# Split weights stored woven in pairs of k-tiles, and strip matmuls run from the last column to the first

## The chip, the core and the metric

The kernel runs on one core of one Trainium2 chip. The metric is the device time of one launch in microseconds. The core has a matmul engine (TensorE, PE in the rows; its weight loads are listed apart as PEld), VectorE (DVE), ScalarE (ACT), GpSimd (POOL) and SyncE (SP), which issues most of the transfers. All share the on-chip memory SBUF; matmuls write to PSUM.

## The reference, cut to what matters

The kernel computes one step of a hybrid decoder layer for 272 prompt rows (256 and 16 meta rows in front) and 8 sample rows, in float32:

```
h = rmsnorm(x, norm1_g);  z = h @ w_in                      # 2048 x 16400 weights
a_out = bg * causal_dwconv(cg * u);  b_out = sigmoid(o) * mlstm(q, k, v, gates)
x = x + (sigmoid(g_a) * a_out + sigmoid(g_b) * b_out) @ w_out
h2 = rmsnorm(x, norm2_g)
up = causal_dwconv(h2 @ w_up)                               # 2048 x 11264 weights
x = x + (silu(up[..., D_FF:]) * up[..., :D_FF]) @ w_down    # 5632 x 2048 weights
y = rmsnorm(x, norm_f_g)
```

Nearly all work is in the four weight products. Each weight element is used for 264 to 280 columns (tokens).

## The kernel before, in words

Every product is cut into **strips**: 128 output features for all tokens, accumulated in one PSUM bank (`bank[0]` to `bank[3]`). A strip's weights come in **units** of up to 8 k-tiles of 128x128 (`KU` = 8; in the down product a strip is 8, 8 and 6 k-tiles). Four units are in flight: `w_raw`, `w_hi` and `w_lo` have four slots of 8·128 columns each (`RING` = 4).

A unit goes through three steps. SP loads it into its slot of `w_raw` (`load`, waits until the unit that was four before has its `w_lo`). ScalarE rounds it to the matmul's reduced format, fp32r, into `w_hi` (`split_hi`, waits for the load and for `unit_used`, that is, until TensorE has finished the unit four before). VectorE subtracts and writes the rest to `w_lo` (`split_lo`). The tokens are split in the same way into `xh`/`xl`, `mh`/`ml` or `hh`/`hl`. TensorE then does, for each k-tile of the unit, hi weights with hi tokens (L1520), then for each hi weights with lo tokens (L1524), then lo weights with hi tokens (L1528): 24 matmuls for a unit of 8 (`unit`). Each matmul has a weight load of 128 columns of its own.

In `w_hi` and `w_lo` a k-tile is 128 adjacent columns, as in `w_raw`; the token tiles are read from column `c0` up, and the bank is written from column 0 up.

The stages in order: a prologue of about 34 us with the first units, which other engines than usual split (`first_hi`, `first_lo_part` on TensorE, L1028 and L1035 on VectorE, L489 and L493 on GpSimd, L730 and L731 on ScalarE); 8 heads of 16 strips of `w_in`, each with a `front` (280 columns for three strips) and a `back` (268 columns); 16 strips of `w_out` (266); then twice 44 strips of `w_up` (268) and 16 strips of `w_down` (264). VectorE also empties the banks (`take`, L987) and does the convolutions; its instructions run in the order in which they are written, with `step` calls for the weights put between the others. Nothing is scheduled by a planner: the order on every engine is written out by hand.

Of the kernel before, what the change touches and what calls it, by code (L numbers as in the profile page):

```python
# [6 lines left out]
def hybrid_decoder_step(nc, ins, outs, scratch_rows, scratch_v, scratch_q):  # L7
# [10 lines left out]
    f32, f32r = mybir.dt.float32, mybir.dt.float32r  # L18
    ALU, ACT = mybir.AluOpType, mybir.ActivationFunctionType
# [7 lines left out]
    P = 128  # L27
# [9 lines left out]
    KT = D // P  # L37
    FT = DFF // P
    TP = NMETA + SEQ
    NT = TP + NS  # L40
# [25 lines left out]
    KU = 8  # L66
# [37 lines left out]
    with ctx:  # L104
        def sb(name, shape, dt=f32):
            return ctx.enter_context(nc.sbuf_tensor(name, shape, dt))

        def sem(name):
            return ctx.enter_context(nc.semaphore(name))
# [3 lines left out]
        xh = sb("xh", [P, KT, NT], f32r)  # L113
        xl = sb("xl", [P, KT, NT], f32r)
        w_raw = sb("w_raw", [P, RING, KU * P])
        w_hi = sb("w_hi", [P, RING, KU * P], f32r)
        w_lo = sb("w_lo", [P, RING, KU * P], f32r)
# [173 lines left out]
        bank = [ctx.enter_context(nc.psum_tensor(f"strip{i}", [P, 512], f32)) for i in range(RING)]  # L291
# [4 lines left out]
        hi_done = sem("hi_done")  # L296
# [6 lines left out]
        half_hi, first_lo, mp_done, bias_done = sem("half_hi"), sem("first_lo"), sem("mp_done"), sem("bias_done")  # L303
# [61 lines left out]
        def col(c, j):  # L365
            return vecs[:, bass.ds(c * KT + j, 1)]


        @block.sync
        def _(sp):  # L370
# [100 lines left out]
        def _(g):  # L471
# [14 lines left out]
            g.memset(gws[:, :, :].bitcast(f32), 0.0).then_inc(gw_split, 1)  # L486
            g.wait_ge(hi_done, 2)
            g.wait_ge(first_lo, 1)
            g.tensor_tensor(w_lo[:, 2, :], w_raw[:, 2, :], w_hi[:, 2, :].bitcast(f32), ALU.subtract)\  # L489
             .then_inc(first_lo, 1)  # L490
            for i, u in enumerate((1, 3)):
                g.wait_ge(hi_done, i + 3)
                g.tensor_tensor(w_lo[:, u, :], w_raw[:, u, :], w_hi[:, u, :].bitcast(f32), ALU.subtract)\  # L493
                 .then_inc(lo_done, 2)

            g.wait_ge(gates_in, 16)
# [152 lines left out]
            for m in range(KT):  # L649
# [5 lines left out]
                if m < NQ:  # L655
                    p = slice(m * Q, (m + 1) * Q)
# [48 lines left out]
        def _(act):  # L705
            def split_hi(u, slot, n16):
                act.wait_ge(unit_landed[slot], n16)
                act.wait_ge(unit_used, u + 1)
                act.activation(w_hi[:, slot, :], w_raw[:, slot, :], ACT.Copy).then_inc(hi_done, 1)  # L709

            def step(n, per, base_u, i):

                u4 = n * per + (base_u + i + RING)
                split_hi(u4, i % RING, n * (16 * per // RING) + 16 * ((base_u + i) // RING + 2))
# [9 lines left out]
            for k in range(KT):  # L724
                act.wait_ge(x_turned, k + 1)
                act.activation(xh[:, k, :], x_bank[k % 6][:, 0:NT], ACT.Copy, scale=vecs[:, k:k + 1])\
                 .then_inc(xh_done, 1)
                if k == 3:
                    act.wait_ge(unit_landed[0], 16)
                    act.activation(w_hi[:, 0, 0:KU * P // 2], w_raw[:, 0, 0:KU * P // 2], ACT.Copy).then_inc(half_hi, 1)  # L730
                    act.activation(w_hi[:, 0, KU * P // 2:], w_raw[:, 0, KU * P // 2:], ACT.Copy).then_inc(hi_done, 1)  # L731
                for kept in (k - 2, k) if k % 4 == 3 else ():
                    act.wait_ge(xl_done, kept + 1)
                    act.activation(xres[:, kept, :], x_bank[kept % 6][:, 0:NT], ACT.Copy).then_inc(x_copied, 1)
                if k == 7:
                    act.wait_ge(hi_done, 2)
                    split_hi(1, 1, 16)
# [237 lines left out]
        def _(v):  # L975
            def split_lo(u, slot):
                v.wait_ge(hi_done, u + 1)
                v.tensor_tensor(w_lo[:, slot, :], w_raw[:, slot, :], w_hi[:, slot, :].bitcast(f32),  # L978
                                ALU.subtract).then_inc(lo_done, 1)

            def step(n, per, base_u, i):
                split_lo(n * per + (base_u + i + RING), i % RING)
# [35 lines left out]
            for k in range(KT):  # L1018
                v.wait_ge(xh_done, k + 1)
                v.scalar_tensor_tensor(out=xl[:, k, :], in0=x_bank[k % 6][:, 0:NT], scalar=vecs[:, k:k + 1],  # L1020
                                       in1=xh[:, k, :].bitcast(f32), op0=ALU.mult, op1=ALU.subtract)\
                                        .then_inc(xl_done, 1)
                if k % 2 == 1:
                    v.tensor_copy(xres[:, k - 1, :], x_bank[(k - 1) % 6][:, 0:NT]).then_inc(x_kept, 1)
                if k == 3:
                    v.wait_ge(half_hi, 1)
                    v.wait_ge(hi_done, 1)
                    v.tensor_tensor(w_lo[:, 0, :], w_raw[:, 0, :], w_hi[:, 0, :].bitcast(f32), ALU.subtract)\  # L1028
                     .then_inc(first_lo, 1)
                if k in (3, 11):  # L1030
                    u = 2 if k == 3 else 3
                    v.wait_ge(unit_landed[u], 16)
                    if k == 11:
                        v.wait_ge(hi_done, 3)
                    v.tensor_scalar(w_hi[:, u, :], w_raw[:, u, :], 1.0, None, ALU.mult).then_inc(hi_done, 1)  # L1035
            v.wait_ge(lo_done, RING + 4)
            v.wait_ge(ssq_done, 3)
            v.wait_ge(msq_clear, 1)
# [358 lines left out]
        def _(pe):  # L1397
# [43 lines left out]
            def first_hi(s, lo, hi):  # L1441
                c0 = C0 if s == 0 else 0
                for k in range(lo, hi):
                    if s == 0 and k == 0:
                        pe.wait_ge(half_hi, 1)
                    elif k % KU == 0 or (s == 0 and k == 4):
                        pe.wait_ge(hi_done, 1 + s + 2 * (k // KU))
                    pe.wait_ge(xl_done, k + 1)
                    w = slice(k % KU * P, (k % KU + 1) * P)
                    for t, xt in enumerate((xh, xl)):  # L1450
                        mm = pe.matmul(bank[s][:, 0:NT - c0], w_hi[:, 2 * s + k // KU, w], xt[:, k, c0:NT],  # L1451
                                       start=(k == 0 and t == 0), stop=False)
                return mm

            def first_lo_part(s, lo, hi, last=False):
                c0 = C0 if s == 0 else 0
                h = lo // KU
                if h == 0:
                    pe.wait_ge(first_lo, s + 1)
                else:  # L1460
                    pe.wait_ge(lo_done, RING + 2 * (s + 1))
                for k in range(lo, hi):
                    pe.wait_ge(xh_done, k + 1)
                    mm = pe.matmul(bank[s][:, 0:NT - c0], w_lo[:, 2 * s + h, (k - h * KU) * P:(k - h * KU + 1) * P],  # L1464
                                   xh[:, k, c0:NT], start=False, stop=(last and k == KT - 1))
                return mm

            def gates(lo, hi):
# [6 lines left out]
            turn_x(0, 4)  # L1475
            warm(6)
            first_hi(0, 0, 4)
            turn_x(4, 8)
            first_lo_part(0, 0, 4)
            first_hi(1, 0, 4)  # L1480
            first_hi(0, 4, 6)
            first_lo_part(0, 4, 8)
            first_hi(0, 6, 8).then_inc(unit_used, 1)
            first_lo_part(1, 0, 4)
            turn_x(8, 12)
            first_hi(1, 4, 8)
# [24 lines left out]
            def unit(u, slot, b, k0, kk, rh, rl, c0, c1, first, last, waits=(), frees=1):  # L1511


                pe.wait_ge(hi_done, u + 1)
                for k in range(kk):
                    for at_k, sm, value in waits:
                        if at_k == k:
                            pe.wait_ge(sm, value)
                    w = slice(k * P, (k + 1) * P)
                    pe.matmul(bank[b][:, 0:c1 - c0], w_hi[:, slot, w], rh[:, k0 + k, c0:c1],  # L1520
                              start=(first and k == 0), stop=False)
                for k in range(kk):
                    w = slice(k * P, (k + 1) * P)
                    pe.matmul(bank[b][:, 0:c1 - c0], w_hi[:, slot, w], rl[:, k0 + k, c0:c1], start=False, stop=False)  # L1524
                pe.wait_ge(lo_done, u + 1 + RING)
                for k in range(kk):
                    w = slice(k * P, (k + 1) * P)
                    mm = pe.matmul(bank[b][:, 0:c1 - c0], w_lo[:, slot, w], rh[:, k0 + k, c0:c1],  # L1528
                                   start=False, stop=(last and k == kk - 1))
                if frees:  # L1530
                    mm.then_inc(unit_used, frees)
# [226 lines left out]
```

## Time and profile before

| | us |
|---|---|
| median of 3 runs | 1708.52 |
| lowest, highest | 1707.7, 1710.4 |
| span of the profiled execution (first to last instruction) | 1706.3 |
| TensorE busy in it | 1695.1 |
| VectorE busy in it | 1200.1 |
| ScalarE busy in it | 766.5 |
| GpSimd busy in it | 479.6 |

The profiled execution has no time of its own beside its span; the median of the runs is 2.2 us above that span. A matmul's row spans its whole way through the engine, so rows of neighbours overlap; the distance from start to start tells what one costs in a stream.

### The profile page before, as it was taken

The page shows a single profiled execution, that of the slowest core. Times are in us where ns is not written, and L with a number is a line of the kernel's source. Part 1 is how long each engine was busy: PE and PEld are TensorE (multiplying, and loading weights), DVE is VectorE, ACT ScalarE, POOL GpSimd, SP SyncE. Part 2 cuts the span into 40 slices and gives each one's busy share as a digit, 9 for nine tenths or more (in the row PEclk, how much of TensorE's full clock was granted, in tenths as well). Part 3 has the DMA queues.
Part 4 walks back from the last instruction along what each step waited for, and adds up shares of the span by engine and source line. Part 5 has one row for each costly group of instructions (what it writes and reads, how often), then busy time and mean ns, then how long its engine had stood idle before and what let it go on. Part 6 is the DMA issues. An engine that isn't in the chain of part 4 may idle for free.

```text
span 1706.3 us, 37177 instructions
## 1 busy us (share of the span) xinstructions
PE 1695.1 (99%) x13726; PEld 1688.7 (99%) x13726; DVE 1200.1 (70%) x1901; ACT 766.5 (45%) x916; POOL 479.6 (28%) x501
## 2 busy tenths in 40 slices
PE   9999999999999999999999999999999999999997
PEld 8999999999999999999999999999999999999997
DVE  5875957667595766759688877777555777777554
ACT  6545435354443535444444554544333334334443
POOL 4422414242141424215343222222000222222220
PEclk9999999999999999999999999999999999999999
DMA  8787786868778586877866666656666666666663
GB/s 204 183 230 197 201 212 155 225 162 231 188 198 212 156 226 163 230 189 199 196 178 182 185 175 175 180 173 173 183 181 181 181 178 179 176 180 177 183 176 119
DMA packets 591165, 318.80 MB, mean 187 GB/s; under 512 B 17684, under 2 KB 585988, under 8 KB 588988
## 3 DMA queue, kind: packets, MB, share of 16 engines
q1 hardware_dynamic: 578564, 292.99, 63.2%
q10 hardware_dynamic: 10448, 21.57, 4.7%
q0 software_dynamic: 2064, 2.92, 0.8%
q8 instruction: 72, 1.18, 0.3%
q14 instruction: 17, 0.14, 0.0%
HBM read 305.09 MB, written 12.78 MB: 186 GB/s over the span
## 4 chain that ended last, share of the span: by engine, by line
PE 99%; ACT 0%; POOL 0%; DVE 0%; issue 0%; ACTq 0%; POOLq 0%; DVEq 0%
PE strip L1528 32%; PE strip L1520 32%; PE strip L1524 32%; PE aux L1399 1%; PE aux L1407 1%; PE strip L1451 0%; PE aux L1581 0%; PE aux L1471 0%; PE strip L1464 0%; PE aux L1611 0%; PE aux L1610 0%; PE aux L1624 0%; PE strip L1399 0%; PE aux L1615 0%; PE aux L1608 0%; PE aux L1616 0%
## 5 line engine op out<-in xcount | busy, mean ns | idle before, releaser
L978 DVE TENSOR_TENSOR w_lo<-w_raw,w_hi 128x1024 fp32r<-128x1024 f32 x556 | 723.1, 1303 | 315.3 <-ACT w_hi L709 314.8
L709 ACT ACTIVATE w_hi<-w_raw 128x1024 fp32r<-128x1024 f32 x557 | 586.1, 1059 | 756.7 <-PE strip L1528 724.7
L1520 PE MATMUL strip<-xh,w_hi 128*128 128x268 f32 (+1 forms) x3424 | 493.1, 286 | 0.0
L1528 PE MATMUL strip<-xh,w_lo 128*128 128x268 f32 (+1 forms) x3424 | 492.4, 286 | 0.0
L1524 PE MATMUL strip<-xl,w_hi 128*128 128x268 f32 (+1 forms) x3424 | 492.0, 286 | 0.0
L1528 PEld LDWEIGHTS strip<-xh,w_lo 128*128 128x128 f32 x3424 | 449.4, 188 | 0.3
L1520 PEld LDWEIGHTS strip<-xh,w_hi 128*128 128x128 f32 x3424 | 449.4, 188 | 0.2
L1524 PEld LDWEIGHTS strip<-xl,w_hi 128*128 128x128 f32 x3424 | 449.4, 188 | 0.0
L680 POOL TENSOR_TENSOR gg<-sg,cz 128x264 f32<-128x264 f32 x44 | 57.1, 1297 | 415.8 <-ACT sg L923 415.8
L1520 PE MATMUL strip<-hh,w_hi 128*128 128x264 f32 x704 | 102.2, 286 | 0.0
L683 POOL TENSOR_TENSOR hid<-gg,cz 128x264 f32<-128x264 f32 x44 | 73.5, 1670 | 102.2 <-DVE cz L1327 102.2
L1528 PE MATMUL strip<-hh,w_lo 128*128 128x264 f32 x704 | 101.3, 285 | 0.0
L1524 PE MATMUL strip<-hl,w_hi 128*128 128x264 f32 x704 | 101.2, 284 | 0.0
L1528 PEld LDWEIGHTS strip<-hh,w_lo 128*128 128x128 f32 x704 | 92.2, 189 | 0.0
L1524 PEld LDWEIGHTS strip<-hl,w_hi 128*128 128x128 f32 x704 | 91.9, 188 | 0.0
L1520 PEld LDWEIGHTS strip<-hh,w_hi 128*128 128x128 f32 x704 | 91.7, 188 | 0.0
L620 POOL TENSOR_TENSOR so<-so,sbm 128x266 f32<-128x266 f32 x16 | 20.6, 1287 | 137.1 <-ACT sbm L881 137.1
L987 DVE TENSOR_TENSOR zs<-strip,rbc 128x266 f32<-128x266 f32 x88 | 38.0, 431 | 26.6 <-PE strip L1528 26.6
L1319 DVE SCALAR_TENSOR_TENSOR cz<-zs,vecs,cz 128x256 f32<-128x256 f32 x88 | 42.7, 485 | 12.9 <-DVE cz L1316 1.8
L611 POOL TENSOR_TENSOR c_st<-c_st,kv 128x512 f32<-128x512 f32 x32 | 49.5, 1545 | 6.5 <-ACT c_st L864 4.5
L606 POOL TENSOR_TENSOR kv<-vg,qkd_g 128x512 f32<-128x512 f32 x32 | 49.2, 1538 | 2.6 <-DMA vg<-scratch_v 0.6
L1327 DVE SCALAR_TENSOR_TENSOR cz<-zs,vecs,cz 128x256 f32<-128x256 f32 x88 | 42.7, 485 | 6.0
(324 smaller groups left out, 1285.3 us busy)
## 6 DMA issues: line engine op xcount, KB each, us to landing
w_raw<-in_w_in SPq DMA_DIRECT2D x256, 512.0 KB, 4.4
w_raw<-in_w_up SPq DMA_DIRECT2D x176, 512.0 KB, 3.9
w_raw<-in_w_down SPq DMA_DIRECT2D x64, 512.0 KB, 3.9
w_raw<-in_w_out SPq DMA_DIRECT2D x32, 512.0 KB, 4.4
w_raw<-in_w_down SPq DMA_DIRECT2D x32, 384.0 KB, 3.3
out<-c_st ACTq DMA_DIRECT2D x8, 1024.0 KB, 7.2
c_st<-in_state_mlstm_C ACTq DMA_DIRECT2D x7, 1024.0 KB, 10.5
rb<-scratch_rows ACTq DMA_DIRECT2D x8, 270.0 KB, 5.0
```

Source lines behind the costliest of these rows:

```text
L606: g.tensor_tensor(kv[:, :, :], vg[:, :].unsqueeze(1).broadcast_to([P, 2, DV]), kw_p.unsqueeze(2).broadcast_to([P, 2, DV]), ALU.mult).then_ ...
L611: g.tensor_tensor(c_p, c_p, kv[:, :, :], ALU.add).then_inc(c_updated, 1)
L680: g.tensor_tensor(gg[:, :], sg[:, :], cz[:, 0, :], ALU.mult).then_inc(gg_done, 1)
L683: g.tensor_tensor(hid[:, :], gg[:, :], cz[:, 1, :], ALU.mult).then_inc(hid_done, 1)
L709: act.activation(w_hi[:, slot, :], w_raw[:, slot, :], ACT.Copy).then_inc(hi_done, 1)
L978: v.tensor_tensor(w_lo[:, slot, :], w_raw[:, slot, :], w_hi[:, slot, :].bitcast(f32), ALU.subtract).then_inc(lo_done, 1)
L987: v.tensor_tensor(out, bank[b][:, c0 - from_c:c0 - from_c + width], rbc[:, c0:c0 + width], ALU.mult).then_inc(evacuated, 1)
L1319: v.scalar_tensor_tensor(out=cz[:, z, 0:SEQ], in0=zs[:, z, 1:1 + SEQ], scalar=wcol[1], in1=cz[:, z, 0:SEQ], op0=ALU.mult, op1=ALU.add)\
L1327: v.scalar_tensor_tensor(out=cz[:, z, 0:SEQ], in0=zs[:, z, 0:SEQ], scalar=wcol[0], in1=cz[:, z, 0:SEQ], op0=ALU.mult, op1=ALU.add)\
L1520: pe.matmul(bank[b][:, 0:c1 - c0], w_hi[:, slot, w], rh[:, k0 + k, c0:c1], start=(first and k == 0), stop=False)
L1524: pe.matmul(bank[b][:, 0:c1 - c0], w_hi[:, slot, w], rl[:, k0 + k, c0:c1], start=False, stop=False)
L1528: mm = pe.matmul(bank[b][:, 0:c1 - c0], w_lo[:, slot, w], rh[:, k0 + k, c0:c1], start=False, stop=(last and k == kk - 1))
```

## The change

Two edits of layout and of order inside instructions, neither of which adds, removes or moves an instruction: each engine's list has the same length and order as before (1568 instructions as written for TensorE, 724 for VectorE, 407 for ScalarE, 230 for GpSimd, 291 for SyncE, loops counted once).

1. **Woven weights.** In `w_hi` and `w_lo` two neighbouring k-tiles share 256 columns: the even k-tile has the even columns, the odd one the odd columns. Whoever writes them (ScalarE, VectorE, at the start GpSimd) writes each k-tile with a step of 2 elements, which is 8 bytes, and reads `w_raw` in sequence as before. VectorE and GpSimd also read `w_hi` with step 2. TensorE loads each weight tile with step 2.
2. **Descending strips.** In every strip matmul the moving rows (the tokens) are read from the last column to the first, and the output is written from the last column to the first, both with a step of -1.

Transfers, `w_raw`, all other matmuls and all waits stay. The diff, cut where lines repeat the pattern:

```diff
+        def plain(t, slot, k0=0, k1=KU):
+            return t[:, slot, k0 * P:k1 * P].rearrange("p (j e n) -> p j e n", e=2, n=P)
+
+        def woven(t, slot, k0=0, k1=KU):
+            return t[:, slot, k0 * P:k1 * P].rearrange("p (j n e) -> p j e n", e=2, n=P)
+
+        def weights(t, slot, k):
+            return t[:, slot, k // 2 * 2 * P:(k // 2 + 1) * 2 * P].rearrange("p (n e) -> p e n", e=2)[:, k % 2, :]
...
@@ split_hi, on ScalarE
-                act.activation(w_hi[:, slot, :], w_raw[:, slot, :], ACT.Copy).then_inc(hi_done, 1)
+                act.activation(woven(w_hi, slot), plain(w_raw, slot), ACT.Copy).then_inc(hi_done, 1)
...
@@ split_lo, on VectorE
-                v.tensor_tensor(w_lo[:, slot, :], w_raw[:, slot, :], w_hi[:, slot, :].bitcast(f32),
+                v.tensor_tensor(woven(w_lo, slot), plain(w_raw, slot), woven(w_hi, slot).bitcast(f32),
                                 ALU.subtract).then_inc(lo_done, 1)
...
@@ the prologue, on VectorE (the splits on GpSimd and ScalarE there alike)
-                    v.tensor_scalar(w_hi[:, u, :], w_raw[:, u, :], 1.0, None, ALU.mult).then_inc(hi_done, 1)
+                    v.tensor_scalar(woven(w_hi, u), plain(w_raw, u), 1.0, None, ALU.mult).then_inc(hi_done, 1)
...
@@ unit, on TensorE (first_hi and first_lo_part alike)
-                    w = slice(k * P, (k + 1) * P)
-                    pe.matmul(bank[b][:, 0:c1 - c0], w_hi[:, slot, w], rh[:, k0 + k, c0:c1],
+                    pe.matmul(bank[b][:, 0:c1 - c0][:, ::-1], weights(w_hi, slot, k), rh[:, k0 + k, c0:c1][:, ::-1],
                               start=(first and k == 0), stop=False)
...
-                    mm = pe.matmul(bank[b][:, 0:c1 - c0], w_lo[:, slot, w], rh[:, k0 + k, c0:c1],
+                    mm = pe.matmul(bank[b][:, 0:c1 - c0][:, ::-1], weights(w_lo, slot, k), rh[:, k0 + k, c0:c1][:, ::-1],
                                    start=False, stop=(last and k == kk - 1))
```

## Rows read from the trace of the kernel before

**Rows 1.** The page, part 1: busy time, share of the span, instructions.

```profile
PE 1695.1 (99%) x13726; PEld 1688.7 (99%) x13726; DVE 1200.1 (70%) x1901; ACT 766.5 (45%) x916; POOL 479.6 (28%) x501
```

**Rows 2.** The page, part 4: the chain that ended last, by engine.

```profile
PE 99%; ACT 0%; POOL 0%; DVE 0%; issue 0%; ACTq 0%; POOLq 0%; DVEq 0%
```

**Rows 3.** Timeline of PE, second w_up stage: start, length, what, count.

```profile
1500.63 1.14 PE L1528 MATMUL strip<-xh,w_lo 128*128 128x268 f32 x8
...
1503.56 1.14 PE L1528 MATMUL strip<-xh,w_lo 128*128 128x268 f32 x8
```

**Rows 4.** Timeline of PE, first w_up stage, the same work.

```profile
1000.29 1.16 PE L1528 MATMUL strip<-xh,w_lo 128*128 128x268 f32 x8
...
1003.27 1.16 PE L1528 MATMUL strip<-xh,w_lo 128*128 128x268 f32 x8
```

**Rows 5.** Groups by line and shape, PEld: count, busy us, mean ns of one.

```profile
L1524 PEld LDWEIGHTS strip<-xl,w_hi 128*128 128x128 f32 x3424 | 449.4, 188 | 0.0
...
L1528 PEld LDWEIGHTS strip<-hh,w_lo 128*128 128x128 f32 x704 | 92.2, 189 | 0.0
...
L1528 PEld LDWEIGHTS strip<-mh,w_lo 128*128 128x128 f32 x256 | 33.2, 188 | 0.0
...
L1399 PEld LDWEIGHTS aux<-ident,xg 128*128 128x128 f32 x32 | 4.1, 142 | 0.0
...
L1581 PEld LDWEIGHTS aux<-q_t,tails 128*16 128x16 f32 x16 | 0.9, 94 | 1.2
```

**Rows 6.** Timeline, end of the run: weight loads for matmuls of one column.

```profile
1694.75 0.75 PEld L1708 LDWEIGHTS aux<-ones,acc 128*128 128x128 f32 x6
```

**Rows 7.** The page, part 5: the two splits, busy us, mean ns.

```profile
L978 DVE TENSOR_TENSOR w_lo<-w_raw,w_hi 128x1024 fp32r<-128x1024 f32 x556 | 723.1, 1303 | 315.3 <-ACT w_hi L709 314.8
L709 ACT ACTIVATE w_hi<-w_raw 128x1024 fp32r<-128x1024 f32 x557 | 586.1, 1059 | 756.7 <-PE strip L1528 724.7
```

**Rows 8.** Groups by line and shape, ACT: a split of half the size.

```profile
L731 ACT ACTIVATE w_hi<-w_raw 128x512 fp32r<-128x512 f32 x1 | 0.6, 642 | 0.0
```

**Rows 9.** Line L978 alone: duration ns, minimum, median, maximum.

```profile
L978 DVE TENSOR_TENSOR w_lo<-w_raw,w_hi x556: 1183/1225/2873, 32.5 to 1685.6; 128x1024 fp32r<-128x1024 f32 x186
```

**Rows 10.** Groups by line and shape, DVE: stepped and unstepped small ones.

```profile
L1313 DVE TENSOR_SCALAR up_last<-zs 128x10 f32 x88 | 15.7, 178 | 13.1 <-DVE zs L987 3.7
...
L1323 DVE TENSOR_TENSOR cz<-cz,pre_f 128x8 f32<-128x8 f32 x88 | 14.1, 160 | 0.0
...
L1015 DVE TENSOR_REDUCE sel<-ident 128x8 f32<-128x128 f32 x1 | 0.4, 383 | 2.8 <-POOL tails L484 2.8
...
L1363 DVE TENSOR_TENSOR x<-strip,xres 128x128 f32<-128x128 f32 x1 | 0.3, 292 | 7.2 <-PE strip L1528 7.2
```

**Rows 11.** Windows, all engines: heads, w_out, second w_up; busy us of each engine.

```profile
330.00:846.00 516.00, 516.00 (x4180) 514.69 (x4179) 362.36 (x508) 232.19 (x295) 169.89 (x185) 1.00 0.76 195
850.00:900.00 50.00, 50.00 (x413) 50.00 (x412) 41.35 (x56) 21.10 (x26) 20.53 (x21) 1.00 0.70 186
...
1310.00:1560.00 250.00, 250.00 (x2050) 250.00 (x2050) 197.27 (x385) 96.79 (x106) 66.20 (x42) 1.00 0.61 178
```

**Rows 12.** The same windows, busy time of L978 alone.

```profile
330.00:846.00 516.00, 225.91 (x166) 1.00 0.76 195
850.00:900.00 50.00, 24.04 (x17) 1.00 0.70 186
...
1310.00:1560.00 250.00, 103.34 (x85) 1.00 0.61 178
```

**Rows 13.** The page, part 6: the weights' transfers, KB each, us from issue to landing.

```profile
w_raw<-in_w_in SPq DMA_DIRECT2D x256, 512.0 KB, 4.4
```

**Rows 14.** Line L1035, the split on DVE in the prologue.

```profile
L1035 DVE TENSOR_SCALAR w_hi<-w_raw x2: 685/688/690, 13.8 to 22.3; 128x1024 fp32r<-128x1024 f32 x2
```

**Rows 15.** Timeline of POOL in the prologue: the split after it.

```profile
14.61 2.39 POOL L489 TENSOR_TENSOR w_lo<-w_raw,w_hi 128x1024 fp32r<-128x1024 f32 x1 [10.39 <-DVE w_hi L1035]
```

**Rows 16.** The chain, prologue: the matmuls that take that split.

```profile
18.12 0.52 PE strip L1464 x4
```

More of the change, by code:

```diff
@@ L488, in _ @@
             g.wait_ge(first_lo, 1)
-            g.tensor_tensor(w_lo[:, 2, :], w_raw[:, 2, :], w_hi[:, 2, :].bitcast(f32), ALU.subtract)\
+            g.tensor_tensor(woven(w_lo, 2), plain(w_raw, 2), woven(w_hi, 2).bitcast(f32), ALU.subtract)\
              .then_inc(first_lo, 1)
@@ L492, in _ @@
                 g.wait_ge(hi_done, i + 3)
-                g.tensor_tensor(w_lo[:, u, :], w_raw[:, u, :], w_hi[:, u, :].bitcast(f32), ALU.subtract)\
+                g.tensor_tensor(woven(w_lo, u), plain(w_raw, u), woven(w_hi, u).bitcast(f32), ALU.subtract)\
                  .then_inc(lo_done, 2)
@@ L729, in _ @@
                     act.wait_ge(unit_landed[0], 16)
-                    act.activation(w_hi[:, 0, 0:KU * P // 2], w_raw[:, 0, 0:KU * P // 2], ACT.Copy).then_inc(half_hi, 1)
-                    act.activation(w_hi[:, 0, KU * P // 2:], w_raw[:, 0, KU * P // 2:], ACT.Copy).then_inc(hi_done, 1)
+                    act.activation(woven(w_hi, 0, 0, KU // 2), plain(w_raw, 0, 0, KU // 2), ACT.Copy).then_inc(half_hi, 1)
+                    act.activation(woven(w_hi, 0, KU // 2), plain(w_raw, 0, KU // 2), ACT.Copy).then_inc(hi_done, 1)
                 for kept in (k - 2, k) if k % 4 == 3 else ():
@@ L1027, in _ @@
                     v.wait_ge(hi_done, 1)
-                    v.tensor_tensor(w_lo[:, 0, :], w_raw[:, 0, :], w_hi[:, 0, :].bitcast(f32), ALU.subtract)\
+                    v.tensor_tensor(woven(w_lo, 0), plain(w_raw, 0), woven(w_hi, 0).bitcast(f32), ALU.subtract)\
                      .then_inc(first_lo, 1)
@@ L1448, in first_hi @@
                     pe.wait_ge(xl_done, k + 1)
-                    w = slice(k % KU * P, (k % KU + 1) * P)
                     for t, xt in enumerate((xh, xl)):
-                        mm = pe.matmul(bank[s][:, 0:NT - c0], w_hi[:, 2 * s + k // KU, w], xt[:, k, c0:NT],
+                        mm = pe.matmul(bank[s][:, 0:NT - c0][:, ::-1], weights(w_hi, 2 * s + k // KU, k % KU), xt[:, k, c0:NT][:, ::-1],
                                        start=(k == 0 and t == 0), stop=False)
@@ L1463, in first_lo_part @@
                     pe.wait_ge(xh_done, k + 1)
-                    mm = pe.matmul(bank[s][:, 0:NT - c0], w_lo[:, 2 * s + h, (k - h * KU) * P:(k - h * KU + 1) * P],
-                                   xh[:, k, c0:NT], start=False, stop=(last and k == KT - 1))
+                    mm = pe.matmul(bank[s][:, 0:NT - c0][:, ::-1], weights(w_lo, 2 * s + h, k - h * KU),
+                                   xh[:, k, c0:NT][:, ::-1], start=False, stop=(last and k == KT - 1))
                 return mm
@@ L1518, in unit @@
                             pe.wait_ge(sm, value)
-                    w = slice(k * P, (k + 1) * P)
-                    pe.matmul(bank[b][:, 0:c1 - c0], w_hi[:, slot, w], rh[:, k0 + k, c0:c1],
+                    pe.matmul(bank[b][:, 0:c1 - c0][:, ::-1], weights(w_hi, slot, k), rh[:, k0 + k, c0:c1][:, ::-1],
                               start=(first and k == 0), stop=False)
                 for k in range(kk):
-                    w = slice(k * P, (k + 1) * P)
-                    pe.matmul(bank[b][:, 0:c1 - c0], w_hi[:, slot, w], rl[:, k0 + k, c0:c1], start=False, stop=False)
+                    pe.matmul(bank[b][:, 0:c1 - c0][:, ::-1], weights(w_hi, slot, k), rl[:, k0 + k, c0:c1][:, ::-1], start=False, stop=False)
                 pe.wait_ge(lo_done, u + 1 + RING)
                 for k in range(kk):
-                    w = slice(k * P, (k + 1) * P)
-                    mm = pe.matmul(bank[b][:, 0:c1 - c0], w_lo[:, slot, w], rh[:, k0 + k, c0:c1],
+                    mm = pe.matmul(bank[b][:, 0:c1 - c0][:, ::-1], weights(w_lo, slot, k), rh[:, k0 + k, c0:c1][:, ::-1],
                                    start=False, stop=(last and k == kk - 1))
```

## The prediction

> **What bounds the kernel now.** I read the shares of busy time first [rows 1]: TensorE is at 99%, VectorE at 70%, ScalarE at 45%. The chain that ended last says the same from the other side, 99% of it is TensorE [rows 2]. So every nanosecond of a strip matmul counts at once, and what the other engines do counts only if it makes TensorE wait.
>
> How long is one strip matmul in the stream? In the second w_up stage 24 of them, one unit, take 1503.56 - 1500.63 = 2.93 us, which is 122.1 ns each, for 268 columns [rows 3]. In the first w_up stage the same work takes 2.98 us or 124.2 ns [rows 4]. There are 3 x (3424 + 704 + 256) = 13,152 strip matmuls outside the prologue, one weight load each [rows 5]; at 122 to 124 ns they fill 1,606 to 1,633 us of the span of 1706.3. One nanosecond on each is 13.2 us, 0.8% of the time. The granted clock is 1.00 throughout, the 2.4 GHz level [rows 11]. At that level 268 columns at one per cycle are 111.7 ns, so 10.4 ns of the 122.1 are something else.
>
> **The edits on TensorE.** Three streams of its change: the weight load (step 2), the moving read (step -1) and the bank write (step -1). No row of before shows any of them with such a step, so each is bounded.
>
> Weight load. It takes 188 ns for 128 columns and 94 ns for 16 [rows 5]: (188 - 94)/112 = 0.84 ns a column, 107 ns for a tile. It isn't limited by what the memory gives: in the transposes the same 128 columns of 4 bytes take 142 ns, (142 - 94)/112 = 0.43 ns a column [rows 5]. In the strips the load thus takes words at half the rate at which that port can deliver adjacent ones. With a step of 2 half of what is fetched goes unused, and the half that is left is just the rate needed. Lower bound 0. Upper bound: a column costs twice as much, 107 ns more. Loads in a row without long matmuls stand (750 - 189)/5 = 112 ns apart [rows 6], 10 ns under the 122.1 of a strip matmul; so the first 10 ns of any growth are hidden and the rest is not: 112 + 107 - 122 = 97 ns each, 13,152 times, +1,276 us. I take 0, because of the reserve of a factor of two, and keep the other as a rival.
>
> Moving read and bank write. Here no reserve shows: they run at 268 columns in 122.1 ns. Adjacent words stay adjacent, all spans have even lengths (264, 266, 268, 280) and start at even columns, so that any aligned pair of words that was fetched or written together is still a pair, met in the other order. Lower bound 0. Upper bound: pairs are no longer joined and a column costs two cycles, 111.7 ns more, 13,152 times, +1,469 us. I take 0, as the set of words touched in each pair of columns is the same; between the ends there is no row to lean on, so this is the largest single risk.
>
> The Trainium skill speaks against this edit: "PSUM — Partial Sum Buffer", Specifications, has cachelines of 8 bytes in PSUM and says that any non-contiguous access pattern slows matmuls significantly. If a step of -1 counts as non-contiguous there, the time is that of the upper bound. No row of this trace shows a bank written with a step.
>
> **The edits on ScalarE and VectorE.** Per unit ScalarE writes 1024 woven elements: 1059 ns, and 642 for 512 [rows 7, 8], (1059 - 642)/512 = 0.81 ns an element. If a stepped write doubles that, a split takes 1.89 us; 557 of them add 463 us and ScalarE stands at 1,230 of 1,706 us, still not the bound. It waits 725 us for TensorE to free slots [rows 7], and a slot turns round in 4 x 2.93 = 11.7 us, against 1.06 + 1.23 + 4.4 us for hi, lo and the next transfer [rows 7, 9, 13]. Even with 1.89 + 1.95 + 4.4 = 8.2 us there are 3.5 us to spare. So: nothing on the path, whichever bound holds. What hides it is the four slots.
>
> VectorE reads one woven stream and writes another: 1,225 ns at the median [rows 9]. Lower bound of the change 0. Two rows of before have steps. The reduction L1015 reads 128 elements at a step of 32 bytes in 383 ns, where 128 adjacent ones take 292 ns in L1363: 0.71 ns an element more [rows 10], which makes a split 1.95 us. L1313 writes 10 elements at a step of 384 bytes in 178 ns, where 8 adjacent ones take 160 in L1323: (178 - 160 - 2)/10 = 1.6 ns more, 2.86 us a split [rows 10]. How much can VectorE bear? In the second w_up stage it is busy 197.3 of 250 us, 103.3 of that in 85 splits [rows 11, 12]; the rest, 94 us, leaves (250 - 94)/85 = 1.83 us for a split. In the w_out stage (50 - 17.3)/17 = 1.92 us, in the heads (516 - 136.5)/166 = 2.29 us. So up to 1.83 us nothing happens, and that is the point from which this decides.
>
> I take 0 here too. A step of 8 bytes touches every 16 bytes twice, the stepped rows above touch each piece of 32 bytes or more once; only in the latter does each word cost an access of its own for certain. The Trainium skill has both sides. "SBUF — State Buffer", section "Door 1: The DMA port swizzle", gives cachelines of 16 bytes and full bandwidth with at least two hits in each: by it a step of two floats is free for all engines. "Vector Engine (DVE) Microarchitecture Reference", section 5.2, measured that runs must be two adjacent words on an 8-byte boundary, 1.71 to 1.98 ns per column otherwise; an estimate from it is 1.98 x 1.024 + 0.16 = 2.2 us a split, over every budget above except the heads'. The trace has no row with a step of 8 bytes that would settle it.
>
> **The prologue.** L1035 splits 1024 elements in 688 ns [rows 14], faster per element than L978, a rate that a stepped write may lose; then it takes about 1.23 us, 0.54 more, twice. GpSimd's split behind the first one starts at 14.61 and takes 2.39 us [rows 15]: 0.54 later it ends at 17.5, and TensorE takes its result at 18.12 [rows 16]. Nothing. If GpSimd's three splits also double, TensorE waits about 2 us for each, 5 us at most. I take 0.
>
> **Sum.** 0 + 0 + 0 + 0 against the span of 1706.3 and the 2.2 us that lie around it up to the median of the runs: 1708.5 us. Its own range: the one variation of the stream that the trace shows without any change of shape is the 2.1 ns between [rows 3] and [rows 4]. Should the first w_up stage (44 strips of 48 matmuls) lose it, that is -4.4 us; should all others gain it, 11,040 x 2.1 ns = +23 us. So 1,704 to 1,732.
>
> **The rivals.**
>
> *Descending streams aren't joined in pairs* (slower). Place: every strip matmul, stage by stage alike. Price 111.7 ns each, 1708.5 + 1,469 = 3,178 us; it decides from the first nanosecond, as nothing hides it. For it: no reserve in the stream, and the page on PSUM. Against it: the words of a pair stay the same. 0.14.
>
> *Woven weights halve the load* (slower): 1708.5 + 1,276 = 2,985 us. For it: the load is only 10 ns from being the limit. Against it: the transposes' rate. 0.03.
>
> *VectorE becomes the bound* (slower). Place: the w_up stages first, then w_out. With 1.95 us a split, (1.95 - 1.83) x 4 splits x 44 pairs of strips = 21 us, and its in-order waits there, which would come on top, are at most about as much again; w_out 1 us: 1,730 to 1,755, say 1,745. With 2.2 us: 65 + 9 us and the waits, up to 1,810. The far end, 2.86 us, would be 181 us in w_up, 146 in the heads and some 50 elsewhere, 2,090. For it: two streams with a step on the engine that has the least room. Against it: two words of every 16 bytes are used. 0.13.
>
> *The 10.4 ns above the column rate come from streams that disturb each other, and the new orders part them* (faster). If half go, 5.2 x 13,152 = -68 us, 1,640 us. For it: they are there, and they differ by stage. Against it: nothing says that order matters. 0.03.
>
> **How the numbers follow.** My forecast, no stream that counts is slower, has 0.67. A difference of 0.2%, 3.4 us, is about what a measurement can tell from none; it is 0.26 ns on a matmul. Within the forecast I give 0.50 to less than that, 0.11 to slower and 0.06 to faster. With the rivals: same 0.50, slower 0.11 + 0.14 + 0.03 + 0.13 = 0.41, faster 0.06 + 0.03 = 0.09. The predicted time is 1708.5. The range holds the forecast and the rival on VectorE up to its 2.2 us, and leaves out the two large losses and the gain, 0.20: 1,697 to 1,812.
>
> **What would show it.** Right: units of 24 matmuls still 2.93 us in the second w_up stage, weight loads still 188 ns, L978 near 1.23 and L709 near 1.06 us, chain 99% TensorE. Weight loads at about 295 ns show the second rival. Units of about 5.6 us with loads still at 188 ns show the first. L978 above 1.83 us, TensorE idle behind it in w_up and the granted clock perhaps falling there show the third. L978 between 1.3 and 1.8 us with unchanged time would mean that the step costs and room hid it. What would make the prediction wrong is above all a cost per column in the descending streams, for which the trace before offers no row at all.

## The result: 5 us slower, all of it in the stream of strip matmuls

| | before | after |
|---|---|---|
| median, us (8 runs each) | 1709.29 | 1714.09 |
| lowest to highest | 1707.7 to 1710.4 | 1713.04 to 1714.43 |
| span of the profiled execution | 1706.3 | 1712.3 |
| ratio of the runs | | 1.0029, 95% interval 1.0019 to 1.0039 |

The forecast was no change, 1708.5. The loss is small, but clear of it: the interval doesn't reach 1. Executions of the kernel before have spans from 1705.6 to 1709.1 us, so the span of one profiled execution can be up to 3 us off from the next; the profiled one here, 1706.3, is a low one, and the runs put the loss at 4.8 us. The page of the changed kernel, busy time and chain, answers to [rows 1, 2]:

```profile
PE 1701.1 (99%) x13726; PEld 1694.7 (99%) x13726; DVE 1199.0 (70%) x1901; ACT 838.9 (49%) x916; POOL 481.3 (28%) x501
...
PE 99%; ACT 0%; POOL 0%; DVE 0%; issue 0%; ACTq 0%; POOLq 0%; DVEq 0%
```

TensorE gained 6.0 us of busy time and the span 6.0 us; it still waits for nobody to speak of. So the question is what a matmul costs in the stream. The timelines of TensorE in the second and the first w_up stage, which answer to [rows 3, 4] (start, length, line, shape, count):

```profile
1500.68 1.15 PE L1533 MATMUL strip<-xh,w_lo 128*128 128x268 f32 x8
...
1503.63 1.03 PE L1533 MATMUL strip<-xh,w_lo 128*128 128x268 f32 x7
```

```profile
1000.98 1.15 PE L1533 MATMUL strip<-xh,w_lo 128*128 128x268 f32 x8
...
1003.93 0.53 PE L1533 MATMUL strip<-xh,w_lo 128*128 128x268 f32 x3
```

Both stages now take 2.95 us for 24 matmuls, 122.9 ns each. Before, they took 122.1 and 124.2. One became slower, the other faster. The w_out stage lost most per matmul. First the kernel before, then the changed one:

```profile
861.92 1.14 PE L1520 MATMUL strip<-mh,w_hi 128*128 128x266 f32 x8
...
864.84 1.14 PE L1520 MATMUL strip<-mh,w_hi 128*128 128x266 f32 x8
```

```profile
862.39 1.15 PE L1527 MATMUL strip<-mh,w_hi 128*128 128x266 f32 x8
...
865.36 0.91 PE L1527 MATMUL strip<-mh,w_hi 128*128 128x266 f32 x6
```

2.92 us against 2.97 for a unit of 24. The weight loads, by line and shape (count, busy us, mean ns), answer to [rows 5], and the two splits to [rows 7] (the third line is L987 alone, minimum, median, maximum, to [rows 9]):

```profile
L1530 PEld LDWEIGHTS strip<-xl,w_hi 128*128 128x128 f32 x3424 | 454.2, 195 | 0.0
```

```profile
L718 ACT ACTIVATE w_hi<-w_raw 128x1024 fp32r<-128x1024 f32 x557 | 660.9, 1194 | 699.9 <-PE strip L1533 657.2
L987 DVE TENSOR_TENSOR w_lo<-w_raw,w_hi 128x1024 fp32r<-128x1024 f32 x556 | 723.6, 1304 | 330.6 <-ACT w_hi L718 330.0
...
L987 DVE TENSOR_TENSOR w_lo<-w_raw,w_hi x556: 1182/1227/2867, 32.8 to 1691.7; 128x1024 fp32r<-128x1024 f32 x186
```

A load takes 195 ns instead of 188. ScalarE's split takes 1194 ns instead of 1059, hidden, since that engine still waits 657 us for TensorE. VectorE's split, with two stepped streams, takes what it took: 1227 ns for 1225 at the median.

Read over all groups of 8 or 6 matmuls in the timelines, with the slowest and fastest twentieth left out, the stages stand so. This table is the tool for everything below; ns per matmul, and us for the span.

| kernel | heads, 280 | heads, 268 | w_out | w_up 1 | w_down 1 | w_up 2 | w_down 2 | span |
|---|---|---|---|---|---|---|---|---|
| matmuls | 1104 | 4944 | 768 | 2112 | 1056 | 2112 | 1056 | |
| before | 128.7 | 122.4 | 121.6 | 124.1 | 121.3 | 122.1 | 122.2 | 1706.3 |
| after | 129.2 | 123.4 | 123.8 | 122.9 | 121.2 | 122.9 | 121.8 | 1712.3 |
| woven only | 130.8 | 123.9 | 125.0 | 123.8 | 122.9 | 123.8 | 123.6 | 1725.0 |
| descending only | 129.2 | 122.6 | 123.8 | 123.3 | 121.6 | 123.4 | 122.3 | 1709.9 |
| stepped load only | 130.8 | 123.9 | 125.0 | 123.8 | 122.9 | 123.9 | 123.6 | 1725.1 |
| woven writes only | 128.7 | 122.4 | 121.6 | 124.1 | 121.3 | 122.1 | 122.2 | 1707.3 |
| descending reads only | 129.1 | 122.5 | 123.8 | 123.4 | 121.6 | 123.3 | 122.3 | 1710.3 |

Row "after" less row "before", times the counts: 0.6 + 4.9 + 1.7 - 2.5 - 0.1 + 1.7 - 0.4 = 5.9 us, against 6.0 of the spans. The account closes. It is less exact elsewhere: for the kernel with descending strips alone it gives 4.7 us where the two profiled spans are 3.6 apart.

### The profile page after: what moved, and what is told of

It is laid out like the page before. It is cut to its first block, busy times and chain, and to the rows that moved or that the text cites. A ratio compares the mean times of both kernels' runs of the same rounds, so it can differ in the third digit from the quotient of the medians.

```text
span 1712.3 us, 37177 instructions
## 1 busy us (share of the span) xinstructions
PE 1701.1 (99%) x13726; PEld 1694.7 (99%) x13726; DVE 1199.0 (70%) x1901; ACT 838.9 (49%) x916; POOL 481.3 (28%) x501
## 3 DMA queue, kind: packets, MB, share of 16 engines
q0 software_dynamic: 2064, 2.92, 0.8%
## 4 chain that ended last, share of the span: by engine, by line
PE 99%; ACT 0%; POOL 0%; DVE 0%; issue 0%; ACTq 0%; POOLq 0%; DVEq 0%
PE strip L1533 32%; PE strip L1527 32%; PE strip L1530 32%; PE aux L1408 1%; PE aux L1416 1%; PE strip L1459 0%; PE aux L1586 0%; PE aux L1479 0%; PE strip L1472 0%; PE aux L1616 0%; PE aux L1615 0%; PE aux L1629 0%; PE strip L1408 0%; PE aux L1622 0%; PE aux L1621 0%; PE aux L1620 0%
## 5 line engine op out<-in xcount | busy, mean ns | idle before, releaser
L718 ACT ACTIVATE w_hi<-w_raw 128x1024 fp32r<-128x1024 f32 x557 | 660.9, 1194 | 699.9 <-PE strip L1533 657.2
L987 DVE TENSOR_TENSOR w_lo<-w_raw,w_hi 128x1024 fp32r<-128x1024 f32 x556 | 723.6, 1304 | 330.6 <-ACT w_hi L718 330.0
L1533 PEld LDWEIGHTS strip<-xh,w_lo 128*128 128x128 f32 x3424 | 454.1, 195 | 0.4 <-DVE w_lo L987 0.4
L1527 PEld LDWEIGHTS strip<-xh,w_hi 128*128 128x128 f32 x3424 | 454.3, 195 | 0.2
L1530 PEld LDWEIGHTS strip<-xl,w_hi 128*128 128x128 f32 x3424 | 454.2, 195 | 0.0
```

The source lines that it names most:

```text
L718: act.activation(woven(w_hi, slot), plain(w_raw, slot), ACT.Copy).then_inc(hi_done, 1)
L987: v.tensor_tensor(woven(w_lo, slot), plain(w_raw, slot), woven(w_hi, slot).bitcast(f32), ALU.subtract).then_inc(lo_done, 1)
L1527: pe.matmul(bank[b][:, 0:c1 - c0][:, ::-1], weights(w_hi, slot, k), rh[:, k0 + k, c0:c1][:, ::-1], start=(first and k == 0), stop=False)
L1530: pe.matmul(bank[b][:, 0:c1 - c0][:, ::-1], weights(w_hi, slot, k), rl[:, k0 + k, c0:c1][:, ::-1], start=False, stop=False)
L1533: mm = pe.matmul(bank[b][:, 0:c1 - c0][:, ::-1], weights(w_lo, slot, k), rh[:, k0 + k, c0:c1][:, ::-1], start=False, stop=(last and k == k ...
```

## Which edit, and which half of it

Three theories stand against each other. W: the weight load, 7 ns longer with its step of 2, lengthens the stream. D: the descending streams do. A: the stepped writes of ScalarE disturb TensorE's reads. Four kernels each keep one part of the change.

**Woven weights, strips ascending again:**

```diff
-                    pe.matmul(bank[b][:, 0:c1 - c0][:, ::-1], weights(w_hi, slot, k), rh[:, k0 + k, c0:c1][:, ::-1],
+                    pe.matmul(bank[b][:, 0:c1 - c0], weights(w_hi, slot, k), rh[:, k0 + k, c0:c1],
```

> The changed kernel with its strip matmuls ascending again; the weights stay woven. Theory W (the weight load, 195 instead of 188 ns with its step of 2, is what lengthens the stream): the same as the changed kernel, span about 1712, w_out stage 123.9 ns per matmul, second w_up stage 122.9, weight loads 195 ns. Theory D (the descending streams cost): the span of the kernel before, about 1706, w_out 121.6 and second w_up 122.1 ns, although the loads still read 195 ns. ScalarE's split 1.19 us by both.

Measured: 1726.29 us, 1.0101 of the kernel before (1.0084 to 1.0118), span 1725.0. Neither theory had this: woven weights alone cost 17 us, three and a half times what the whole change costs.

**Descending strips, weights plain:**

```diff
         def woven(t, slot, k0=0, k1=KU):
-            return t[:, slot, k0 * P:k1 * P].rearrange("p (j n e) -> p j e n", e=2, n=P)
+            return t[:, slot, k0 * P:k1 * P].rearrange("p (j e n) -> p j e n", e=2, n=P)
         def weights(t, slot, k):
-            return t[:, slot, k // 2 * 2 * P:(k // 2 + 1) * 2 * P].rearrange("p (n e) -> p e n", e=2)[:, k % 2, :]
+            return t[:, slot, k * P:(k + 1) * P]
```

> The kernel before with descending strips; the weights stay plain. Theory W: the span of the kernel before, about 1706, weight loads 188 ns, w_out 121.6 ns per matmul, first w_up stage 124.1. Theory D: span about 1712, w_out 123.9, second w_up 122.9 ns. If one of the two edits makes the first w_up stage faster (124.1 to 122.9 in the changed kernel), one of these two runs shows which.

Measured: 1711.74 us, 1.0020 (1.0009 to 1.0030), span 1709.9, loads 188 ns. So the descending strips cost some 3 us alone by the runs (4.7 by the stages), which theory W had at 0. 17 and 3 don't add up to 5: with woven loads, the descending strips take 12.7 us of span off (1725.0 to 1712.3).

**The stepped load alone** (the second run's first hunk with the changed kernel's `weights`, strips ascending):

> Ascending strips; TensorE loads its weights with step 2, but ScalarE, VectorE and GpSimd write and read them plain, so each matmul multiplies with a mixture of two k-tiles and the outputs are not the reference's. Theory W: as the changed kernel, loads 195 ns, w_out 123.9 ns per matmul, span about 1712, with ScalarE's split at 1.06 us. Theory A (ScalarE's stepped writes, which take 1.19 us for 1.06, disturb TensorE's reads): loads and matmuls as before, 188 ns and 121.6, span about 1706.

**The woven writes alone** (the changed kernel's `woven` with plain `weights`, strips ascending):

> Ascending strips; the weights are written woven, but TensorE loads 128 adjacent columns, so each matmul multiplies with a mixture of two k-tiles and the outputs are not the reference's. Theory W: as the kernel before, span about 1706, loads 188 ns, although ScalarE's split takes 1.19 us. Theory A: as the changed kernel, loads longer than 188 ns, w_out 123.9, span about 1712.

Measured: 1726.65 us (1.0104, 1.0087 to 1.0120) and 1709.44 us (1.0003, 0.9993 to 1.0012). In the table the stepped load has the stages of the woven-only kernel and the woven writes those of the kernel before, to 0.1 ns. The rows of ScalarE's split in the two, first the stepped load, then the woven writes:

```profile
L718 ACT ACTIVATE w_hi<-w_raw x557: 1040/1061/1067, 17.6 to 1703.0; 128x1024 fp32r<-128x1024 f32 x186
```

```profile
L718 ACT ACTIVATE w_hi<-w_raw x557: 1104/1142/1217, 17.1 to 1685.6; 128x1024 fp32r<-128x1024 f32 x186
```

The kernel with the unchanged split has the loss, the one with the longer split has none. Theory A falls; the 17 us come with TensorE's own stepped read of its weights.

**Descending reads, bank written ascending:**

```diff
-                    pe.matmul(bank[b][:, 0:c1 - c0][:, ::-1], weights(w_hi, slot, k), rh[:, k0 + k, c0:c1][:, ::-1],
+                    pe.matmul(bank[b][:, 0:c1 - c0], weights(w_hi, slot, k), rh[:, k0 + k, c0:c1][:, ::-1],
```

> Plain weights; the moving rows are read from the last column down, the bank is written ascending, so every strip's columns come out mirrored and the outputs are not the reference's. If the read is what the descending strips change, the stages are those of the run with both descending: w_out 123.8 ns, first w_up 123.3, second 123.4, span 1710. If it is the write to the bank, they are those of the kernel before: 121.6, 124.1, 122.1, span 1706.

Measured: 1712.88 us, 1.0030 (1.0019 to 1.0040), span 1710.3. That is 5.0 us above the kernel before of the same series. Every stage is within 0.1 ns of the kernel with both descending. The write to the bank from the last column down is free in these stages; what descending does, it does by the read.

## Does the load's length explain it?

With woven weights loads became 7 ns longer, and the stages' distances changed by -0.3 to +3.4 ns. To see the load by itself, the strip matmuls were cut to 128 and to 240 columns, with plain and with woven weights (the other tokens left out):

```diff
-                    pe.matmul(bank[b][:, 0:c1 - c0], weights(w_hi, slot, k), rh[:, k0 + k, c0:c1],
+                    pe.matmul(bank[b][:, 0:P], weights(w_hi, slot, k), rh[:, k0 + k, c0:c0 + P],
```

> The kernel before with strip matmuls of 128 columns instead of 264 to 280 outside the prologue; the other tokens are left out, so most outputs are not computed. It shows how far apart the weight loads alone can stand. Theory L (the load's own length is the limit of the stream and the step lengthens it): about 122 ns per matmul, no less than the full kernel's, and the woven sister 7 more. Theory C (load and moving stream each fit in less, and disturb each other): about 112 ns, as the loads of the one-column matmuls at the end of the trace before, (750 - 189)/5.

> The same 128 columns with woven weights, ascending. Both theories: loads of 195 ns and a distance about 7 ns longer than the plain sister's, 119 ns by theory C, 129 by theory L. If the distance is the same as the sister's, the 7 ns are delay at the load's start or end and not occupancy, and the loss of the full kernel comes from the two streams meeting.

> The kernel before with 240 columns in each strip matmul outside the prologue (the other tokens are left out). Rows alone would be 100 ns, loads alone stood 112 ns apart with 128 columns. If a stream costs just the longer of its two parts: 112 ns per matmul. If the parts disturb each other: above 112, between that and the 121.3 of 264 columns.

> The same 240 columns with woven weights, ascending. If the cost is the longer of the two parts: 118 ns, 6 more than the plain sister. If it is in the meeting: above 118; and the nearer the rows come to the load's length the smaller the difference to the plain sister, 1.5 to 3.4 ns at 264 to 268 columns.

The timelines, from stretches where the granted clock is 1.00: 128 columns plain, 128 woven (both in w_out), 240 plain, 240 woven (both in w_up 2).

```profile
959.83 1.06 PE L1527 MATMUL strip<-mh,w_hi 128*128 128x128 f32 x8
...
962.51 1.06 PE L1527 MATMUL strip<-mh,w_hi 128*128 128x128 f32 x8
```

```profile
960.91 1.11 PE L1527 MATMUL strip<-mh,w_hi 128*128 128x128 f32 x8
...
963.75 1.11 PE L1527 MATMUL strip<-mh,w_hi 128*128 128x128 f32 x8
```

```profile
1400.05 1.06 PE L1530 MATMUL strip<-xl,w_hi 128*128 128x240 f32 x8
...
1402.74 1.06 PE L1530 MATMUL strip<-xl,w_hi 128*128 128x240 f32 x8
```

```profile
1400.08 1.12 PE L1530 MATMUL strip<-xl,w_hi 128*128 128x240 f32 x8
...
1402.94 1.12 PE L1530 MATMUL strip<-xl,w_hi 128*128 128x240 f32 x8
```

Over 24 matmuls: 111.7, 118.3, 112.1 and 119.2 ns. 128 and 240 columns cost the same, so up to 240 the load is the limit, and its step costs 6.6 to 7.1 ns in these stretches, all or nearly all of its growth. At 264 to 280 columns the stream needs 121 to 129 ns with plain weights, more than either load takes alone. There the longer load should be hidden, if a matmul cost the longer of its two parts. The prediction reckoned so. It isn't: 1.4 to 3.4 ns come through (with w_up 1, where it is -0.3, the exception). So load and rows are not independent when both are near the limit.

That doesn't explain the whole distance. By the prediction's 111.7 ns for 268 columns, the columns alone are 110.0 ns at 264 and 116.7 at 280, and the measured 121.3 and 128.7 are 11 to 12 ns above them. A fixed remainder of that size would bring 240 columns to 111 to 112 ns, which is where the load's limit lies too. No run has the rows without a load for each matmul, so whether the remainder is a cost of the matmul itself or comes from the load stays open.

## How far the step may go

Weaving four k-tiles instead of two makes the step 16 bytes. In `plain`, `woven` and `weights` every 2 became a 4.

> Weights woven from four k-tiles, so that every access has a step of 16 bytes, strips ascending. If a 16-byte piece of memory is what one access fetches, each weight now costs an access of its own: the load's slope doubles, about 107 ns more, loads near 300 ns, about 220 ns per matmul, and a span near 3000 us; VectorE's split about 1.9 us, ScalarE's above 1.6. If instead the load pays per word for any step that is not 1, as the 7 ns of step 2 could also be read, the loads stay at 195 ns and the span near 1725 us, that of the run with step 2.

Measured: 3188.45 us, one run. Loads, the splits (minimum, median, maximum) and two lines of TensorE's timeline:

```profile
L1527 PEld LDWEIGHTS strip<-xh,w_hi 128*128 128x128 f32 x3424 | 845.1, 331 | 0.2
```

```profile
L987 DVE TENSOR_TENSOR w_lo<-w_raw,w_hi x556: 2001/2027/3131, 38.7 to 3157.6; 128x1024 fp32r<-128x1024 f32 x186
...
L718 ACT ACTIVATE w_hi<-w_raw x557: 2022/2057/2106, 18.7 to 3155.6; 128x1024 fp32r<-128x1024 f32 x186
...
1500.51 2.04 PE L1530 MATMUL strip<-xl,w_hi 128*128 128x268 f32 x8
1502.39 2.04 PE L1533 MATMUL strip<-xh,w_lo 128*128 128x268 f32 x8
```

A load takes 331 ns, 143 more than plain, and a matmul 1.88 us / 8 = 235 ns. The cliff lies above 8 and at or below 16 bytes (12 wasn't tried), on all three engines: VectorE's split goes from 1.23 to 2.03 us and ScalarE's from 1.15 to 2.06. That is the rule of the Trainium skill, "SBUF — State Buffer", section "Door 1: The DMA port swizzle": lines of 16 bytes, full bandwidth with at least two hits in each. The runs agree with it: on VectorE a step of 8 bytes cost 2 ns of 1225. Elsewhere it cost less than the step of 16 bytes, but not nothing: ScalarE lost 8 to 13% and the weight load 7 ns. The Trainium skill's "Vector Engine (DVE) Microarchitecture Reference", section 5.2, from which the prediction estimated 2.2 us a split for a step of 8 bytes, is contradicted by the 1.23. A step of 16 bytes comes near it: 2.03 us, of which 0.16 is the fixed part that the estimate took, leave 1.83 ns a column, between the section's 1.71 and 1.98. The same section lists 2.50 ns too, for a step of 24 words; nothing here was that slow. The remark on non-contiguous patterns in the Trainium skill, "PSUM — Partial Sum Buffer", Specifications, doesn't reach a step of -1: the descending write cost nothing.

## Entry or place?

The same loop runs at 124.1 ns in the first w_up stage of the kernel before and at 122.1 in the second. Is it how the stage is entered, or where its tiles lie? A single extra matmul (two rows of 8 columns in the trace), ahead of the first w_up loop:

```diff
+                if c == 0:
+                    pe.matmul(aux[1][:, 0:8], ones[:, :], ident[:, 0:8], start=True, stop=True)
                 with pe.Fori(1 if c == 0 else 0, FC // 2) as i:
```

> The kernel before with one more matmul of 8 columns (ones with the identity, into a spare bank), once, ahead of the loop of the first w_up stage. In the kernel before the same loop runs at 124.1 ns per matmul in its first stage and 122.1 in its second. Theory C with locking (load and rows meet in a pattern that repeats itself, and which pattern a stage falls into depends on how it is entered): the first stage changes its distance, most likely to one of the values seen, 122.1 to 123; at 122.1 it gains 4 us, span 1702. Rival (something in that stage is slower, whatever the entry: the transfers, the loop's place in memory): it stays at 124.1, span 1706.

Measured: 1709.19 us, 1.0003 (0.9994 to 1.0013); all seven stages are those of the kernel before, w_up 1 at 124.1. One push doesn't change the pattern. The rival isn't shown by that either, and why the two stages differ stays open.

The other question was asked by moving the weight slots by 32 bytes, with no access changed. The small tables behind the slots move with them, the token tiles stay:

```diff
         xl = sb("xl", [P, KT, NT], f32r)
+        sb("shift", [P, 8])
         w_raw = sb("w_raw", [P, RING, KU * P])
```

> The kernel before with the weight slots 32 bytes further up in memory; nothing else. If load and rows meet at addresses (the same part of the memory at the same moment), the stages' distances change with the shift in either direction, by 0.5 ns or more in some stage (6 us in all if it were everywhere). If only the order in time matters, all stages keep their values: 122.4, 121.6, 124.1, 121.3, 122.1.

Measured: 1721.41 us in one run, span 1719.7. The second w_up stage of this kernel, against the 2.93 us of [rows 3]:

```profile
1500.03 1.16 PE L1529 MATMUL strip<-xh,w_lo 128*128 128x268 f32 x8
...
1503.01 1.16 PE L1529 MATMUL strip<-xh,w_lo 128*128 128x268 f32 x8
```

2.98 us for a unit, 124.2 ns, as the first stage. The weight loads of this kernel:

```profile
L1529 PEld LDWEIGHTS strip<-xh,w_lo 128*128 128x128 f32 x3424 | 452.3, 188 | 0.7 <-DVE w_lo L979 0.5
```

A kernel that does the same accesses, with loads of the same length, lost 13.4 us of span, twice the loss under study. So four more kernels with shifted slots, 64 and 128 bytes for the kernel before (`[P, 16]`, `[P, 32]`), 32 bytes for the others:

> The kernel before with the weight slots 64 bytes further up. If what counts is the place within 64 bytes, its stages and its span are those of the kernel before (1706). If it is a longer period, the stages differ again from both the kernel before and the one shifted by 32 bytes (1719.7): anything between about 1700 and 1725.

> The kernel before with the weight slots 128 bytes further up. With a period of 64 or 128 bytes the span of the kernel before, 1706; otherwise another value.

> The changed kernel with the weight slots 32 bytes further up. If the 5 us of the change belong to the accesses, it is 5 us above the kernel before with the same shift (1719.7), about 1725. If they are a matter of place, it lands anywhere around the changed kernel's 1712, below the shifted kernel before as likely as above it.

> Woven weights with ascending strips and the weight slots 32 bytes further up. If the load's step costs 17 us whatever the place, it is 17 us above the kernel before with the same shift: 1737. If a woven load, which meets twice as many pieces of memory, averages over places, it stays near its own unshifted 1725.

> Plain weights, descending strips, weight slots 32 bytes further up. If descending reads cost 3 us of themselves: 3 above the shifted kernel before, 1723. If they part load and rows wherever the tiles lie, as they do with woven weights, and only missed the lucky place of the kernel before: below 1719.7, near the unshifted run's 1710.

Spans of the profiled executions by place, us, with the median, ratio and interval of those that were run several times:

| weights, strips | +0 | +32 bytes | +64 | +128 |
|---|---|---|---|---|
| plain, ascending (before) | 1706.3 | 1719.7 | 1711.6 (1712.80; 1.0020, 1.0010 to 1.0029) | 1708.0 |
| plain, descending | 1709.9 | 1713.2 | | |
| woven, descending (the change) | 1712.3 | 1713.7 (1714.66; 1.0031, 1.0019 to 1.0042) | | |
| woven, ascending | 1725.0 | 1725.1 | | |

The stages behind it: in the shifted kernel before, w_up 2 goes from 122.1 to 124.1, the heads from 122.4 to 123.4, w_out from 121.6 to 123.3, w_down 1 from 121.3 to 122.4, and the loads stay at 188 ns. At +64 w_up 2 runs at 124.1 too, at +128 at 122.1 again; w_up 1 is at 124.1 in all four kernels with plain weights and ascending strips. So place decides about the second stage, and the first has something else besides. What follows, within these places:

- With plain weights the stream depends on where the weight slots lie, over 13.4 us. Since the token tiles stayed, the relation of the two is the likely reason; the slots' own address wasn't tried apart from it. Of the four places tried, the kernel before and the one at +128 can't be told apart (1709.77 and, in one run, 1709.73 us), the other two are worse.
- Between the two places tried, the changed kernel's span hardly differs (1712.3 and 1713.7), though w_out goes from 123.8 to 125.0, and the woven, ascending one's not at all. At +32 bytes the changed kernel is 6.0 us below the unchanged one.
- A stepped load with ascending rows costs 5 us at +32 and 19 at +0: both reach the same bad value.
- Descending rows cost 3.6 us of span at +0 and gain 6.5 at +32 with plain weights, and gain 12.7 and 11.4 with woven ones.

That load and moving read meet in memory, and that place and order decide how often, is a reading that fits these rows: the distance moves with the address and with the order of the rows, and the loads' own length doesn't move with either. It is not shown. The meeting itself has no row; which part of an address matters, and why woven weights are insensitive, wasn't tried. None of the kernels that do the whole work beats the one before.

## Point by point

- **What bounds the kernel**: right. TensorE at 99%, nothing else on the chain, one nanosecond 13.2 us. The account by stages closes to 0.1 us.
- **ScalarE and VectorE**: right in time, and on VectorE in size: 1,227 ns, where the rival had 1.95 to 2.2 us. That rival fell. ScalarE's split grew by 0.13 us of the 0.83 allowed for, hidden by its 657 us of waiting, as reckoned.
- **The two large rivals**: neither pairs unjoined (+1,469 us) nor a doubled load (+1,276) came. At a step of 16 bytes the latter is real: 3188 us. The argument from the transposes, that the load uses half of what its port delivers, held at 8 bytes but for 7 ns. The prologue's term of 0 held as well: VectorE's split there took 688 ns as before.
- **The step that failed**: "so the first 10 ns of any growth are hidden". The growth was 7 ns and loads alone stood 118 to 119 ns apart, under 121.3, as the step wanted. Yet 17 us came through with ascending strips. The prediction put two overlapping streams at the longer of the two. Up to 240 columns, where the load is the longer, the distances fit that; at 264 to 280 it doesn't hold, and the slack of 10 ns wasn't slack.
- **The read descending, taken as 0**: right in that no column cost double, as unjoined pairs would, but it has a price of its own, +3 us with plain weights at this place. Over woven weights it gained 12 and offset most of the load's loss. 5 us are what is left of two terms that don't simply add up, one forecast at 0 and 17 in fact, the other forecast at 0 and between +3 and -13. That the sum came out near the forecast is luck.
- **The gain rival** (streams that disturb each other are parted by the new order) had 0.03 and named what these rows fit best. Its sign was wrong for the sum at this place and right for the first w_up stage, 124.1 to 122.9, and for descending rows over woven weights.
- **The forecast's own range**, 1,704 to 1,732 from the 2.1 ns between two stages, held the time. Two errors that were each put at 0 partly cancelled, so that doesn't speak for its terms. The spread between [rows 3] and [rows 4] was the one sign that a stream can have two speeds for one shape. It stood in the prediction as a width of the forecast, and not as a sign that load and rows may not be independent.

## What to carry to other kernels

Where one engine is busy 99% of the time, its two overlapping streams may not hide each other for nothing: a load 8% under the distance of the matmuls (112 of 122 ns) still cost when it grew, so price such a part between zero and its growth, not at zero. For a stepped fp32 stream a step of 8 bytes added 0.2% to the duration on VectorE, 8 to 13% on ScalarE and 4% to the load; one of 16 bytes added 65 to 95% on each. Before crediting or blaming an edit for less than 1% in a matmul stream, shift the tiles by 32 bytes in both kernels: here the shift alone was worth 13 us of span, more than the change.

## What the runs showed of the hardware that was not expected

- The distance of matmuls depends on where the weights lie while the tokens stay: 122.1 or 124.1 ns in the same stage, for 32 bytes.
- With a weight load of 128 columns for each, a matmul of 128 columns costs as much as one of 240: 111.7 and 112.1 ns in the stretches shown, 111.7 and 111.6 over the w_out stage. From there to 264 columns it rises to 121.3, 9 ns for 24 columns, about what the 24 columns take by themselves (10 ns by the 111.7 for 268).
- With 128 columns the granted clock fell in part of the span, and the kernel with plain weights took 2174.9 us, more than the full one. The granted clock by slices of its span, first with plain, then with woven weights:

```profile
PEclk9555899955799999899999965555555555555555
```

```profile
PEclk9989655999895559999999999999999999999998
```

TensorE was busy all the time by its rows, yet in the kernel with plain weights the clock stood at the level of 1.2 GHz from about 1250 us to the end. A window there, and one of the same kernel at the 2.4 GHz level (width, busy us of PE, PEld, DVE, ACT, POOL, then the clock):

```profile
1320.00:1420.00 100.00, 100.00 (x471) 100.00 (x471) 28.76 (x28) 22.29 (x22) 0.00 (x0) 0.50 0.37 105
960.00:966.00 6.00, 6.00 (x56) 6.00 (x55) 4.42 (x6) 4.42 (x6) 2.22 (x2) 1.00 0.70 197
```

471 matmuls in 100 us are 212 ns each, against 112 at the other level. In the kernel before and the changed one the page shows no slice below 9 tenths; the mean clock of both is 0.998. Why the clock fell is open. This is why the four cut kernels are compared by stretches at clock 1.00 and not by their times.
